# Loads of x and of two modulation blocks moved from SyncE's queue to ScalarE's at the start of a two-block kernel

## What is computed

```python
c_act = jax.nn.silu(c)
mod = jnp.dot(c_act, ada_w[l]) + ada_b[l]
sh1, sc1, g1, sh2, sc2, g2 = jnp.split(mod, N_MOD, axis=-1)

h = modulate(rms_norm(x, norm1_g[l]), sh1, sc1)       # h * (1 + scale) + shift
z = jnp.einsum('bsd,de->bse', h, w_in[l]) + b_in[l]
```

## Time and profile before

| | us |
|---|---|
| median of 3 runs | 1394.37 |
| lowest and highest of the 3 | 1393.5 and 1396.28 |
| the profiled execution | 1393.47 |
| its span, first to last instruction | 1391.7 |
| TensorE busy | 1366.7 |
| VectorE busy | 1040.7 |
| ScalarE busy | 888.1 |
| GpSimd busy | 654.1 |

### The profile page before, as it was taken

One profiled execution on the slowest core, in us unless ns is written; L12 is line 12 of the kernel. 1 busy time (PEld: TensorE's weight loads), 2 busy tenths in 40 slices (PEclk: granted clock), 3 DMA queues, 4 the chain that ended last, 5 costly groups with the idle time before them and its releaser, 6 DMA issues.

```text
span 1391.7 us, 32152 instructions
## 1 busy us (share of the span) xinstructions
PE 1366.7 (98%) x9840; PEld 1268.2 (91%) x9840; DVE 1040.7 (75%) x2233; ACT 888.1 (64%) x1861; POOL 654.1 (47%) x503
## 2 busy tenths in 40 slices
PE   7999999999999999999999999999999999999998
PEld 4799999999999978999999999999998888888886
DVE  7778868888978486429999968888876666666665
ACT  5668765555445665547888687777765555555554
POOL 4896782000006857688889887777730000000000
PEclk9999999999999999999999999999999999999998
DMA  9766575988983633565555554444456666566652
GB/s 345 277 244 228 198 256 186 323 320 318 343 318 122 209 121 107 187 222 166 181 182 184 184 175 152 153 161 153 152 166 196 195 191 189 194 196 193 190 191 90
DMA packets 79797, 283.84 MB, mean 204 GB/s; under 512 B 8821, under 2 KB 8949, under 8 KB 79610
## 3 DMA queue, kind: packets, MB, share of 16 engines
q1 hardware_dynamic: 79738, 283.07, 59.3%
HBM read 281.99 MB, written 1.05 MB: 203 GB/s over the span
## 4 chain that ended last, share of the span: by engine, by line
PE 79%; POOL 6%; issue 5%; PEld 3%; DVE 3%; ACT 2%; DMA 1%; PEldq 0%; POOLq 0%; SPq 0%; DVEq 0%; ACTq 0%
PE psA L1822 19%; PE psA L1825 19%; PE psA L1826 19%; POOL w_lo L563 6%; PE psD L1822 6%; PE psD L1825 5%; PE psD L1826 5%; PE psD L2283 1%; PEld psA L1822 1%; PE psD L2284 1%; PEld psA L1826 1%; PEld psA L1825 1%; DVE arena L1541 1%; DMA xT<-x 1%; PEld psD L2240 0%
## 5 line engine op out<-in xcount | busy, mean ns | idle before, releaser
L628 ACT CAST w_hi<-raw 128x512 fp32r<-128x512 f32 x864 | 529.5, 620 | 424.5 <-PE psA L1822 306.8
L563 POOL TENSOR_TENSOR w_lo<-raw,w_hi 128x512 fp32r<-128x512 f32 x476 | 633.3, 1350 | 352.3 <-ACT w_hi L628 341.7
L1822 PE MATMUL psA<-h_hi,w_hi 128*128 128x256 f32 x1568 | 452.8, 289 | 0.6 <-POOL w_lo L563 0.5
L1825 PE MATMUL psA<-h_lo,w_hi 128*128 128x256 f32 x1568 | 443.0, 283 | 0.0
L1826 PE MATMUL psA<-h_hi,w_lo 128*128 128x256 f32 x1568 | 442.9, 282 | 0.0
L1100 DVE TENSOR_TENSOR w_lo<-raw,w_hi 128x512 fp32r<-128x512 f32 x388 | 266.1, 691 | 152.8 <-ACT w_hi L628 151.4
L1822 PEld LDWEIGHTS psA<-h_hi,w_hi 128*128 128x128 f32 x1568 | 300.0, 191 | 4.2 <-issue 1.5
L1825 PEld LDWEIGHTS psA<-h_lo,w_hi 128*128 128x128 f32 x1568 | 300.2, 191 | 0.1
L1826 PEld LDWEIGHTS psA<-h_hi,w_lo 128*128 128x128 f32 x1568 | 299.9, 191 | 0.0
L1822 PE MATMUL psA<-w_hi,u_hi 128*128 128x512 f32 x512 | 199.4, 389 | 0.4 <-DVE u_lo L1163 0.4
L1826 PE MATMUL psA<-w_hi,u_lo 128*128 128x512 f32 x512 | 199.2, 389 | 0.0
(11 more groups left out here) (391 smaller groups left out, 2218.0 us busy)
## 6 DMA issues: line engine op xcount, KB each, us to landing
raw<-expert_down SPq DMA_DIRECT2D x128, 512.0 KB, 3.2
raw<-expert_up SPq DMA_DIRECT2D x128, 512.0 KB, 3.5
arena<-ada SPq DMA_DIRECT2D x96, 512.0 KB, 4.9
raw<-gateup SPq DMA_DIRECT2D x44, 512.0 KB, 5.1
raw<-feat SPq DMA_DIRECT2D x28, 512.0 KB, 4.0
raw<-win SPq DMA_DIRECT2D x24, 512.0 KB, 3.2
raw<-down SPq DMA_DIRECT2D x22, 512.0 KB, 5.9
raw<-wout SPq DMA_DIRECT2D x20, 512.0 KB, 3.3
```

The lines of the kernel that those rows point to most:

```text
L563: nc.gpsimd.tensor_tensor(w_lo[:, s * HALF:(s + 1) * HALF], raw_half(n), w_hi[:, s * HALF:(s + 1) * HALF].bitcast(F32), ALU.subtract).then ...
L628: nc.scalar.copy(w_hi[:, n % SLOTS * HALF:(n % SLOTS + 1) * HALF], raw_half(n)).then_inc(hi_ready, 1)
L1822: first = mm(o, w[0], m[0], start=start, stop=False, skip_group_check=True)
L1825: mm(o, w[0], m[1], start=False, stop=False, skip_group_check=True)
```

## The change

SyncE no longer loads x. ScalarE issues four loads at the very start of its list, ahead of the silu: both halves of x, then ada blocks 0 and 8 (ada[0 * KC] and ada[1 * KC]) into the same places and with the same semaphores as before. SyncE's loop over chunks leaves out the two ada loads of chunk 0 and counts its modulation blocks from 2 on. Everything that waits for these loads waits for the same semaphores.

```diff
-            for z in range(2):
-                sp.dma_start(xT[:, 4 * z:4 * z + 4, :], x[:, 4 * z:4 * z + 4, :]).then_inc(sem(f"x_in{z}"), 16)
...
+            adas.n = 2
             for kc in range(KC):
-                load_ada(ada[kc])
-                load_ada(ada[KC + kc])
+                if kc > 0:
+                    load_ada(ada[kc])
+                    load_ada(ada[KC + kc])
                 load(tok_chunks[:, 0:2, kc // 2, kc % 2 * 512:kc % 2 * 512 + 512], 512)
...
             own = Own(act, sem("act_own"))
+            for z in range(2):
+                act.dma_start(xT[:, 4 * z:4 * z + 4, :], x[:, 4 * z:4 * z + 4, :]).then_inc(sem(f"x_in{z}"), 16)
+            for n in range(2):
+                act.dma_start(ada_place(n), ada[n * KC]).then_inc(ada_full[n], 16)
```

## The result

| | before | after |
|---|---|---|
| median of 20 executions, us | 1393.97 | 1400.22 |
| the profiled execution, us | 1393.47 | 1400.21 |
| its span, us | 1391.7 | 1398.4 |

What follows compares the result with a forecast made beforehand. TensorE's start was taken as the bound, set by x's second half or ada block 8. Late ada block 8 gave +0.3 us, other terms 0: 1393.8 on the profiled execution, 1394.7 on the median; range 1392.1 to 1397.0.

Steps and rivals of the forecast that it cites:

- the +0.3: VectorE's second modulation product waits for ada block 8, landing at 14.2, and starts at 14.3 instead of 14.04: +0.3 us.
- What bounds the kernel: TensorE, busy 98% of the span; its start at 20.00 moves the end, set by x's second half or ada block 8.
- The small tables: cols on SyncE shares engines with x; landing time doubled makes VectorE 2.3 us later, all but 0.9 covered; not added.
- rival 2: Queues take equal turns from the first byte; ada block 8 lands at 16.3: +2.3 us, 1396.7, start near 22.3; chance 0.13.
- Who gets which place: Landing order of loads from two queues: x's second half at 8.9, ada block 0 at 11.4, ada block 8 at 14.2.
- ScalarE's queue goes first throughout: Bounding case for the loads' landings: x's second half at 8.2, ada block 8 at 10.7; -1.4 us.
- Rival 1: ScalarE's loads keep their head start, x's second half lands at 8.2: -1.4 us, 1393.0, start near 18.6; chance 0.17.
- Issuing on ScalarE: Four issues of 0.46 us ahead of ScalarE's first table load; bias split ends at 5.7, costs nothing; upper end 1.4 later.
- Behind 20 us: Later blocks land up to 1.57 us sooner, but TensorE is already fully busy from 24.5 to 28.5: buys nothing there.
- Clock and lengths around the span: Faster TensorE pace shifts: 2.1 us lost or won, chance 0.08; time around the span adds 0, upper end 1.77.

Runs made afterwards that it cites:

- the kernel with the angles later: Against the changed kernel, VectorE's angles moved into its loop at chunk 2, with cols waited for only behind the sums; ratio 1.0061, +6.7 us.

## Why the prediction was wrong

The measured 1400.22 lies above the range (1392.1 to 1397.0), and a time beyond noise on the slow side had a chance of 0.08. With the 3.2 us of the step that failed, below, in place of the +0.3, the sum on the median of 1394.37 would have been 1397.6.

**What bounds the kernel: right as far as it went.** That TensorE's start moves the end by about as much held: +3.76 us of start for 4 us of time. But the part named two supplies that could set the start, x's second half and ada block 8. There was a third. VectorE's first work waits for cols, and the rule above says it was 1.45 us (20.00 - 18.55) from setting the start itself, and 0.85 and 0.3 in the two further profiles of the same kernel (19.45 against 4.44 + 14.16, 18.94 against 4.46 + 14.16).

**The small tables: the step that failed.** The prediction saw the term, the 3.36 us wait and the 1.39 us of idle time that cover it, and even rival 2 mentions the four small loads. It bounded the time to landing at twice the old, so +2.3 and 0.9 behind the cover. It was three times the old: 2.25 became 6.92, +4.67, and +3.2 behind the cover. The doubling had no row behind it; it is what sharing half and half by bytes would give. The runs showed 2.80 us before the first packet of cols, for which the prediction had no term, and 1.58 in turns by packets. An upper end that was available, that cols lands no sooner than the loads it runs with, was left out: cols landed at 8.86, between ada blocks 0 and 8, and at 8.46 where it stood behind x on one queue.

**Who gets which place: wrong.** x's first half landed at 4.99 instead of 6.1, 4.24 us behind its issue, where 5.4 had been carried over from one profile of before (the two further ones have 4.6 and 4.4). ada block 8 was put at 14.2 and landed at 10.19, x's second half at 8.9 and landed at 6.43, both ahead of the end called "ScalarE's queue goes first throughout" (10.7 and 8.2). While SyncE's queue has the small tables at its head, ScalarE's moves 0.42 MB to next to nothing and then 0.45 to 0.16; when SyncE's large loads come up, from about 8 us on, the share turns (0.24 to 0.41 MB) but the four loads are nearly done. VectorE never waited for ada: the +0.3 did not come about.

**Rival 1** (the head start is kept, start near 18.6) had its condition met. ScalarE finished the squares at 9.48, and in before the start came 8.99 us behind their end (20.00 - 11.01); that makes 18.47, and the kernel with the angles later shows 18.53. The gain was there and the wait for cols took its place. **Rival 2** gave the right sign and nearly a right start (22.3), and that is luck: ada block 8, which it made late, landed at 10.19 and not at 16.3. Turns from the first byte did not show (103 packets against 2), and what was held back was the queue with the small tables, which was not ScalarE's.

The Trainium skill's rule of turns (the same section of "DMA: Bandwidth & Descriptors"), weighed there, was applied to two streams of like packets; applied to the tables, whose packets stand in the same round, it would have said which side loses, though by turns of single packets not how much: they cover 1.58 of the 4.67 us.

**Issuing on ScalarE: right.** 0.44 to 0.48 us an issue against the 0.46 taken; c's spreading on TensorE begins at 5.13 instead of 3.41 and ends at 8.88, against the 9.0 forecast and a reader at 16.10. The bias split ended at 7.40 and not at 5.7, since its table was late; nothing on the way to TensorE's start waited for it.

**Behind 20 us: right.** The eighth large transfer lands at 14.94 instead of 17.9, and no time is gained by it.

**Clock and lengths around the span.** The execution is 1.81 us longer than the span, as against 1.77: the second queue costs nothing there. Between 24.5 and 28.5 TensorE started 18 to 20 products in the three profiles of before and 12 to 15 in those of after, since the faster pace comes after a later start; it is part of the shift and no extra.

## What to carry to other kernels

Before moving large loads to a second queue, list what stays on the first and who waits for it: a small table that was ahead of the large loads is afterwards beside them; here its queue nearly stood still at first, and then got as many packets as the other, but small ones. Bound its landing by that of the large loads it runs with, and add all the work behind its first reader to the path before any cover is taken off. If a supply is 1.4 us from being the bound, price it as carefully as the bound itself, and take a second profile of the unchanged kernel before a late difference is put down to a change.

## What was not expected of the hardware

- A load of 1 KB took 1.7 us to land with nothing large in the other queue, 4.0 with x there (after), and 4.9 where x stood in the queue beside (three small tables on ScalarE). One of 168 KB took 2.3, 6.9 in after, and 5.0 in the kernel with x alone on ScalarE.
- With pos alone on the other queue cols took 3.8 us instead of 2.3, although no large load was in that queue. pos is no reason for it: its packets were through by 2.15, ahead of the first of cols. The kernel before with the angles on GpSimd has 3.4 with one queue. In both a few packets (11 and 5 of 128) start about a microsecond behind the others; why is open.
- VectorE's small instructions ran up to five times longer beside a busy GpSimd: 2.74 us for two that take 0.52. The long ones end as a product of GpSimd does (28.49 and 30.47, where GpSimd's end at 28.45 and 30.42), as if they had waited for it.
- The unchanged kernel has two paces of its products from 358 to 418 us, 515 and 502 in 60 us at a granted clock of 1.00 in both. What sets it is open.
